# The scan's inverse in 128-token tiles: carrying a transposed product beside the partial inverse, and emptying its banks on two engines

## Chip, cores and metric

One core of a Trainium2 chip (trn2). The metric is the device time of the whole program in microseconds, the median of three runs; lower is better. TensorE is called PE below, VectorE DVE, ScalarE ACT, GpSimd POOL, SyncE SP.

## The reference, cut to what matters

The program is two model blocks on 1024 tokens of width 1024. The change lies in one stage of the first block, a delta-rule scan over tokens with 16 heads of 64, run forward and backward:

```python
def step(S, inp):
    w_t, k_t, v_t, kk_t, b_t = inp[:5]
    sa = jnp.einsum('bhvk,bhk->bhv', S, kk_t)
    S = (S * w_t[:, :, None, :] - sa[..., None] * b_t[:, :, None, :]
         + v_t[..., None] * k_t[:, :, None, :])
    o = jnp.einsum('bhvk,bhk->bhv', S, inp[5]) if with_out else None
    return S, o
...
for d, (lw, la) in enumerate(...):
    S, o = rwkv7_scan(rh, heads(w), kd, vh, kk, heads(a), S0[d], reverse=(d == 1))
```

The kernel doesn't step through the tokens. It takes tiles of 128 tokens; inside a tile the recurrence is a unit-triangular system of 128 equations per head, whose matrix `tri` is the identity plus the masked products of b and kk. It needs the inverse of `tri`, applied to two right-hand sides, and passes a 64x64 state from tile to tile.

## The kernel before, in words

The stage is the function `rwkv`. It works through 8 pairs of heads (i, `HP`), and for each pair 5 units (n): unit 0 is the context tokens (no output needed), units 1 to 4 the 1024 tokens. A unit takes two tiles for each of two directions (x = 0 forward, 1 backward), so with two heads there are 4 matrices of 128x128 per direction (q = 0 to 3), side by side in one [128, 4, 128] buffer, or in one PSUM bank of 512 columns. A direction owns four of the eight banks (0 to 3 of `bank(x, b)`). There are 40 units, (i, n).

**The levels.** The inverse is built by doubling. `lev0` to `lev6` are constant masks with 1 on the diagonal and -1 in the off-diagonal blocks of size 2^m. Y starts as `tri` masked by lev0 (the inverse of the 2x2 blocks), and X as its transpose. A level m = 1 to 6 does, for each direction:

- `g` (PE, bank 0): G = Mr'X, with Mr a rounded copy of `tri`;
- `join` (DVE, L1529): Gs = bank 0 times the mask lev m, rounded to fp32r;
- `x_next` (PE, bank 1), not in the last level: X = Y'Gs, then `x_out` (ACT, L1182) copies it to X;
- `y_next` (PE, bank 2): Y = Gs'Y, then `y_out` (ACT, L1186) copies it to Y.

Each product is `quad`: four matmuls (L1308), 128 columns wide, with a weight load each. A level is so 24 matmuls over both directions, 2 joins and 4 copies. PE's order within a level is g(0), y_next(1) of the level before, g(1), x_next(0), y_next(0), x_next(1).

**Between the levels of two units** (called the transition below) PE has, in this order: `turn_kv` for the next unit's keys and values (L1260, L1262), the last `y_next` of both directions with `turn_ab` (L1271, L1273), `solve` (Y' times the right-hand sides), `gram_b`, `product` (residual with the unrounded `tri`), `gram_k`, `refine` (one correction with Y), `start` for the next unit (L1299: transpose of Y0 into bank 1; L1302: MakV), `g` of the next unit's level 1, then `passing` (L1380) and the products that pass the state and give the output. DVE has in this order: `masks_b` (L1516, L1518), `residual` (L1533), `masks_k` (L1523, L1525), `refined` (L1537, L1538), `join` of level 1, `passed` (L1544, L1545), `state` (L1551) and, for n > 2, `out` (L1557). ACT has keys_out (L1165), the last y_out, pairs_out, solved, start_out (L1176 the first X; L1178 AMv), and for n = 1, 2 an output copy (L1196). POOL makes Y0 (L1123), Mr (L1124) and Rr (L1127).

**Tails.** The finishing of pair i-1 is spread over pair i. PE does `mean` after level 1 of unit 0 and `variance` after level 1 of unit 1 (L1237, two products of 512 columns each). DVE does `center` (L1489) in level 3 of unit 0, `spread` (L1494) in level 3 of unit 1, `normal` (L1499) in level 2 and `affine` (L1504) in level 4 of unit 2. In the last pair DVE also rotates the first keys of the next stage: one `turn` piece (two 128x512 products, L1576 to L1583) in each of levels 2 to 5 of units 2, 3 and 4.

The order on each engine is written out by hand; engines meet in semaphores (`Marks`: `done` counts, `wait` waits for a named point). An engine serves its list strictly in order.

Of the kernel before, what the change touches and what calls it, by code (L numbers as in the profile page):

```python
# [22 lines left out]
P = 128  # L23
# [930 lines left out]
def rwkv(nc, G, proj, Xd, oa, v_tok, rope):  # L954
# [15 lines left out]
    with nc.cleanup_on_exit(), ExitStack() as ctx:  # L970
# [41 lines left out]
        spare = lambda h: bank(h, 3)  # L1012


        lev = range(1, LEVELS)
        last = LEVELS - 1

        def front_names(n):
            xs = n > 0
            return {"pe": ["T1", "T0", "gB", "gK", "XT", "MakV"], "act": ["Ktok", "Vtok", "Atok", "Btok", "X0", "AMv"],  # L1020
                    "dve": ["tri", "MrbT", "MakT", "MrkT"] if xs else ["tri", "MakT"], "pool": ["Y0", "Mr", "AMr"]}

        def level_names(n):
            xy = sum(([f"X{m}", f"Y{m}"] if m < last else [f"Y{m}"] for m in lev), [])
            return {"pe": sum(([f"G{m}", f"X{m}", f"Y{m}"] if m < last else [f"G{m}", f"Y{m}"] for m in lev), []),
                    "act": xy, "dve": [f"G{m}" for m in lev]}

        def back_names(n):
            xs = n > 0
            return {"pe": ["C0", "MC", "XR", "GQ", "Z0"] + (["O0"] if xs else []) + (["Z1"] if n < 4 else []) + (["O1"] if xs else []),  # L1030
                    "act": ["C0"] + (["O"] if n in (1, 2) else []),
                    "dve": ["R", "W", "nY"] + (["GT"] if xs else []) + ["QT", "S0"] + (["S1"] if n < 4 else []) + (["O"] if n > 2 else [])}

        def marks(kind, names):
            return [{e: Marks(nc, None, f"b_{e}_{kind}{x}", sum(([f"{n}.{q}" for q in names(n)[e]] for n in range(5)), []))
                     for e in names(0)} for x in range(2)]
        F, L, B = marks("front", front_names), marks("level", level_names), marks("back", back_names)
        pe_t = Marks(nc, None, "b_pe_tail", ["mu", "var"])
# [17 lines left out]
        with nc.Block() as block:  # L1056
# [95 lines left out]
            def _(act):  # L1152
# [78 lines left out]
            def _(pe):  # L1231
# [18 lines left out]
                def turn_kv(i, n, x):  # L1250
# [6 lines left out]
                    if i_ >= 0:  # L1257
                        L[x]["act"].wait(pe, i_, f"{n_}.X{last - 1}")
# [52 lines left out]
                def g(i, n, x, m):  # L1311
                    if m == 1:
                        F[x]["act"].wait(pe, i, f"{n}.AMv")
                        F[x]["pool"].wait(pe, i, f"{n}.Mr")
                    else:
                        L[x]["act"].wait(pe, i, f"{n}.X{m - 1}")
                    L[x]["pe"].done(quad(bank(x, 0), Mr[x], X[x]), f"{n}.G{m}")

                def x_next(i, n, x, m):
                    L[x]["dve"].wait(pe, i, f"{n}.G{m}")  # L1320
                    if m > 1:
                        L[x]["act"].wait(pe, i, f"{n}.Y{m - 1}")
                    L[x]["pe"].done(quad(bank(x, 1), Y0[x] if m == 1 else Y[x], Gs[x]), f"{n}.X{m}")

                def y_next(i, n, x, m):
                    i_, n_ = before(i, n)
                    if m == 1 and i_ >= 0:
                        B[x]["dve"].wait(pe, i_, f"{n_}.S1" if n_ < 4 else f"{n_}.S0")
                    if m == last:
                        L[x]["dve"].wait(pe, i, f"{n}.G{m}")  # L1330
                        L[x]["act"].wait(pe, i, f"{n}.Y{m - 1}")
                    L[x]["pe"].done(quad(bank(x, 2), Gs[x], Y0[x] if m == 1 else Y[x]), f"{n}.Y{m}")

                def levels(i, n):
                    for m in lev:
                        if m > 1:
# [13 lines left out]

# [122 lines left out]
            def _(dve):  # L1473
# [1965 lines left out]
```

How the kernel before makes its waits and increments, by code:

```python
    def wait(self, back=0):  # L68
        self.eng.wait_ge(self.sem, self.it * self.per + (self.base + self.n - back))
# [48 lines left out]
    def load(self, eng, src, i, per, l, split=False):  # L118
        if split:
            eng.wait_ge(self.cut, i * per + (self.split_base + l + 1))
        else:
            eng.wait_ge(self.free, i * per + (self.base - self.split_base + l + 1))
        b = (self.base + l) % NBUF
        eng.dma_start(self.buf[:, b], src).then_inc(self.full[b], 16)
# [1 line left out]
    def landed(self, eng, i, per, l):  # L127
        n = self.base + l
        eng.wait_ge(self.full[n % NBUF], i * (16 * per // NBUF) + 16 * (n // NBUF + 1))
        return self.buf[:, n % NBUF]
# [1 line left out]
    def split_hi(self, act, l):  # L133
        n = self.split_base + l
        raw = self.landed(act, 0, 0, l)
        act.wait_ge(self.begun, n + 1)
        self.nc.scalar.activation(self.hl[:, n % NBUF, 0], raw, ACT.Copy).then_inc(self.hi_done, 1)
# [1 line left out]
    def split_lo(self, dve, l):  # L140
        n = self.split_base + l
        hi, lo = self.hl[:, n % NBUF, 0], self.hl[:, n % NBUF, 1]
        dve.wait_ge(self.hi_done, n + 1)
        self.nc.vector.tensor_tensor(lo, self.buf[:, (self.base + l) % NBUF], hi.bitcast(F32), ALU.subtract).then_inc(self.cut, 1)
# [1 line left out]
    def split_first(self, eng, scalar):  # L147
# [6 lines left out]
            self.nc.scalar.activation(hi, raw, ACT.Copy).then_inc(self.hi_done, 1)  # L154
        else:
            eng.wait_ge(self.hi_done, n + 1)
            self.nc.vector.tensor_tensor(lo, raw, hi.bitcast(F32), ALU.subtract).then_inc(self.cut, 1)
```

## Time and profile before

| | |
|---|---|
| Median of 3 runs | 4833.94 us (4833.16 to 4834.51) |
| The profiled execution's span | 4830.5 us |
| Its time outside the span | not shown; the span is 3.4 us under the median |
| Busy, whole program | PE 4675.5 us (97%), DVE 2558.1 (53%), ACT 1869.7 (39%), POOL 429.0 (9%) |
| Granted TensorE clock | full in nearly all of 40 slices, nine tenths in three |
| The scan's stage | 1369.5 to 2750, 1380.5 us for 40 units |

A matmul's record covers the time from its issue to its modelled end, about 0.28 us for 128 columns, and the next is issued before that; so the busy share of PE hides gaps, and the distance between issues is what a product costs. A line x4 of the timeline is four merged instructions: its duration less that of one, divided by three, is the distance of the issues.

### The profile page before, as it was taken

What the parts mean: (1) busy time and instruction counts of PE and PEld (TensorE: products, weight loads), DVE (VectorE), ACT (ScalarE), POOL (GpSimd) and SP (SyncE); (2) the same over time, 40 slices, a digit from 0 to 9 for tenths busy, and PEclk for the clock granted to TensorE, in tenths of its full rate; (3) what the DMA queues carried; (4) which work ended last, traced back from release to release, by engine and by line L of the source; (5) the groups of instructions that cost most, each with busy time, mean ns of one, the idle gap of its engine ahead of it and who ended that gap; (6) DMA issues with size and microseconds to landing.
All of it is one profiled execution on the core that took longest, in us unless ns stands there. A gap on an engine that the chain in (4) does not pass through costs nothing. (4 is left out here: it accounts for less than half of the span.)

```text
span 4830.5 us, 68919 instructions
## 1 busy us (share of the span) xinstructions
PE 4675.5 (97%) x28888; PEld 3832.5 (79%) x28888; DVE 2558.1 (53%) x3722; ACT 1869.7 (39%) x3164; POOL 429.0 (9%) x347
## 2 busy tenths in 40 slices
PE   7999999999999999999999899899999779999999
PEld 5888777778999999999999744488777557888887
DVE  3245555446535555555555577555443755555543
ACT  3234443445435554555455434311333753111111
POOL 0000000000022322232222100000010000000000
PEclk9999999999989999999999899999999899999999
DMA  5333434344410110110112154333120021121222
GB/s 204 115 138 140 145 131 154 138 147 153 148 60 19 41 55 28 57 44 23 61 40 84 35 160 126 125 119 140 48 84 26 14 109 53 70 74 70 87 105 92
DMA packets 155988, 441.93 MB, mean 91 GB/s; under 512 B 17169, under 2 KB 47121, under 8 KB 140449
## 3 DMA queue, kind: packets, MB, share of 16 engines
q1 hardware_dynamic: 140624, 383.98, 22.7%
q0 software_dynamic: 9296, 32.58, 1.9%
q10 hardware_dynamic: 5760, 20.97, 1.2%
q8 instruction: 230, 3.77, 0.3%
q14 instruction: 78, 0.63, 0.0%
HBM read 294.86 MB, written 141.56 MB: 90 GB/s over the span
## 5 line engine op out<-in xcount | busy, mean ns | idle before, releaser
L202 PE MATMUL pr_ps<-uhl,w_split 128*128 128x512 f32 (+1 forms) x1520 | 586.0, 385 | 3.1 <-DVE w_split L145 2.2
L206 PE MATMUL pr_ps<-uhl,w_split 128*128 128x512 f32 (+1 forms) x1520 | 571.3, 376 | 0.0
L205 PE MATMUL pr_ps<-uhl,w_split 128*128 128x512 f32 (+1 forms) x1520 | 570.5, 375 | 0.0
L1529 DVE TENSOR_TENSOR b_G<-b_ps,cst 128x512 fp32r<-128x512 f32 x480 | 331.6, 692 | 358.4 <-PE b_ps L1308 357.8
L138 ACT ACTIVATE w_split<-share 128x2048 fp32r<-128x2048 f32 x64 | 122.6, 1915 | 699.4 <-DVE ou_vc L3264 271.1
L202 PEld LDWEIGHTS pr_ps<-uhl,w_split 128*128 128x128 f32 x1520 | 286.7, 189 | 81.5 <-issue 29.2
L205 PEld LDWEIGHTS pr_ps<-uhl,w_split 128*128 128x128 f32 x1520 | 286.8, 189 | 56.1 <-issue 5.8
L206 PEld LDWEIGHTS pr_ps<-uhl,w_split 128*128 128x128 f32 x1520 | 286.6, 189 | 52.7
L1182 ACT ACTIVATE b_X<-b_ps 128x512 fp32r<-128x512 f32 x400 | 240.1, 600 | 213.7 <-PE b_ps L1308 211.4
L1186 ACT ACTIVATE b_Y<-b_ps 128x512 fp32r<-128x512 f32 x480 | 286.8, 598 | 83.2 <-PE b_ps L1308 83.1
L1308 PE MATMUL b_ps<-b_X,b_Mr 128*128 128x128 f32 x1920 | 313.9, 287 | 1.0
L1308 PE MATMUL b_ps<-b_G,b_Y 128*128 128x128 f32 x1920 | 307.3, 287 | 1.6 <-DVE b_G L1529 1.3
L1308 PE MATMUL b_ps<-b_Y,b_G 128*128 128x128 f32 x1920 | 302.2, 281 | 0.3 <-DVE b_G L1529 0.3
L202 PE MATMUL ou_ps<-ou_a,w_split 128*128 128x512 f32 x704 | 277.0, 393 | 7.7 <-DVE ou_a L2119 7.7
L1123 POOL TENSOR_TENSOR b_Y<-b_tri,cst 128x512 fp32r<-128x512 f32 x80 | 101.8, 1273 | 2001.6 <-DVE b_tri L1516 2001.6
L205 PE MATMUL ou_ps<-ou_a,w_split 128*128 128x512 f32 x704 | 275.2, 391 | 0.0
L206 PE MATMUL ou_ps<-ou_a,w_split 128*128 128x512 f32 x704 | 275.2, 391 | 0.0
L202 PE MATMUL mx_ps<-mx_a,w_split 128*128 128x512 f32 x640 | 259.3, 405 | 13.5 <-DVE mx_a L2119 13.5
L1308 PEld LDWEIGHTS b_ps<-b_G,b_Y 128*128 128x128 f32 x1920 | 253.6, 194 | 22.0 <-issue 15.9
L1308 PEld LDWEIGHTS b_ps<-b_X,b_Mr 128*128 128x128 f32 x1920 | 258.7, 195 | 14.2 <-issue 6.7
L1308 PEld LDWEIGHTS b_ps<-b_Y,b_G 128*128 128x128 f32 x1920 | 259.8, 196 | 0.5 <-DVE b_G L1529 0.5
L776 DVE COPY pr_stage<-pr_ps 128x256 f32<-128x256 f32 (+1 forms) x92 | 49.7, 540 | 391.8 <-PE pr_ps L206 391.6
(490 smaller groups left out, 10088.8 us busy)
## 6 DMA issues: line engine op xcount, KB each, us to landing
w_ring<-in_w_in SPq DMA_DIRECT2D x41, 1024.0 KB, 5.3
proj<-pr_stage SPq DMA_DIRECT2D x160, 256.0 KB, 2.0
share<-in_w_up SPq DMA_DIRECT2D x24, 1024.0 KB, 4.7
ar<-share SPq DMA_DIRECT2D x32, 512.0 KB, 2.8
b_AR<-ar SPq DMA_DIRECT2D x64, 256.0 KB, 2.9
pr_raw<-proj SPq DMA_DIRECT2D x48, 256.5 KB, 3.5
ada<-in_ada_w SPq DMA_DIRECT2D x24, 512.0 KB, 5.6
ff<-ou_vc ACTq DMA_DIRECT2D x24, 512.0 KB, 2.6
```

What stands on the lines that cost most here:

```text
L138: self.nc.scalar.activation(self.hl[:, n % NBUF, 0], raw, ACT.Copy).then_inc(self.hi_done, 1)
L202: mm = nc.tensor.matmul(dst, a[0], b[0], start=start, stop=False)
L205: nc.tensor.matmul(dst, a[0], b[1], start=False, stop=False)
L206: return nc.tensor.matmul(dst, a[1], b[0], start=False, stop=stop)
L776: V.tensor_copy(dst, src).then_inc(taken[1], 1)
L1123: F[x]["pool"].done(tt(Y0[x][:], tri[x][e][:], rep(K("lev0"), 4), ALU.mult), f"{n}.Y0")
L1182: L[x]["act"].done(A(X[x][:], heads(x, 1), ACT.Copy), f"{n}.X{m}")
L1186: L[x]["act"].done(A(Y[x][:], heads(x, 2), ACT.Copy), f"{n}.Y{m}")
L1308: mm = mmul(bk[:, q * P:(q + 1) * P], lhsT[:, q], rhs[:, q], start=True, stop=True)
L1529: L[x]["dve"].done(V.tensor_tensor(Gs[x][:], heads(x, 0), rep(K(f"lev{m}"), 4), ALU.mult), f"{n}.G{m}")
```

## The change

X is no longer kept. In its place E, a product in transposed form, is kept beside Y in one buffer `EY` [128, 4, 2, 128], so that one matmul with 256 moving columns advances both. Gs gets two buffers. A level m = 1 to 4 is then, for each direction:

- `f`: F = E'Gs (128 columns, bank 0; for m = 0 with Mr in place of E), which the next `join` masks into the other Gs;
- `ey`: [E, Y] = Gs'[E, Y] (256 columns, banks 1 and 2; heads 0 and 1 in bank 1, heads 2 and 3 in bank 2);
- bank 1 is copied out by ACT (`low`), bank 2 by DVE (`high`).

Level 5 is F5 and Y5 alone, level 6 is Y6. The transition gets a join of level 0 (from bank 1, after L1299's transpose, which now takes Mr), F0 and E0 in place of `g`, and ACT copies E0 in place of X. POOL makes Mr first and Y0 afterwards, the latter once the previous unit's `refine` has read Y.

```diff
-        X = [sb(f"X{x}", [P, 4, P], F32R) for x in range(2)]
-        Y0 = [sb(f"Y0{x}", [P, 4, P], F32R) for x in range(2)]
-        Y = [sb(f"Y{x}", [P, 4, P], F32R) for x in range(2)]
-        Gs = [sb(f"G{x}", [P, 4, P], F32R) for x in range(2)]
+        EY = [sb(f"EY{x}", [P, 4, 2, P], F32R) for x in range(2)]
+        E, Y = [t[:, :, 0] for t in EY], [t[:, :, 1] for t in EY]
+        Gs = [[sb(f"G{x}{b}", [P, 4, P], F32R) for b in range(2)] for x in range(2)]
...
+        both = lambda x: ps[:, 4 * x + 1:4 * x + 3].rearrange("p b (q a f) -> p (b q) a f", q=2, a=2)
...
+        high_on_dve = lambda x: True
...
                     for x in range(2):
                         F[x]["dve"].wait(pool, i, f"{n}.tri")
-                        F[x]["pool"].done(tt(Y0[x][:], tri[x][e][:], rep(K("lev0"), 4), ALU.mult), f"{n}.Y0")
                         F[x]["pool"].done(ts(Mr[x][:], tri[x][e][:], 1.0, None, ALU.mult), f"{n}.Mr")
+                    for x in range(2):
+                        i_, n_ = before(i, n)
+                        if i_ >= 0:
+                            B[x]["pe"].wait(pool, i_, f"{n_}.XR")
+                        F[x]["pool"].done(tt(Y[x], tri[x][e][:], rep(K("lev0"), 4), ALU.mult), f"{n}.Y0")
...
-                def x_out(i, n, x, m):
-                    L[x]["pe"].wait(act, i, f"{n}.X{m}")
-                    L[x]["act"].done(A(X[x][:], heads(x, 1), ACT.Copy), f"{n}.X{m}")
+                def ey_out(i, n, x, m):
+                    L[x]["pe"].wait(act, i, f"{n}.EY{m}")
+                    L[x]["act"].done(A(EY[x][:, 0:2], both(x)[:, 0:2], ACT.Copy), f"{n}.low{m}")
...
+                def f(i, n, x, m):
+                    L[x]["dve"].wait(pe, i, f"{n}.G{m}")
+                    if m == 0:
+                        F[x]["act"].wait(pe, i, f"{n}.AMv")
+                    elif m == 1:
+                        L[x]["act"].wait(pe, i, f"{n}.E0")
+                    else:
+                        L[x]["act"].wait(pe, i, f"{n}.low{m - 1}")
+                    for q in range(4):
+                        if q == 2 and m > 1:
+                            high(x).wait(pe, i, f"{n}.high{m - 1}")
+                        mm = mmul(bank(x, 0)[:, q * P:(q + 1) * P], E[x][:, q] if m else Mr[x][:, q], Gs[x][m % 2][:, q], start=True, stop=True)
+                    L[x]["pe"].done(mm, f"{n}.F{m}")
...
+                    for q in range(4):
+                        mm = mmul(both(x)[:, q], Gs[x][m % 2][:, q], EY[x][:, q], start=True, stop=True)
+                    L[x]["pe"].done(mm, f"{n}.EY{m}")
...
                 def levels(i, n):
-                    for m in lev:
-                        if m > 1:
-                            g(i, n, 0, m)
-                            y_next(i, n, 1, m - 1)
-                            g(i, n, 1, m)
-                        if m < last:
-                            x_next(i, n, 0, m)
-                            y_next(i, n, 0, m)
-                            x_next(i, n, 1, m)
+                    for m in range(1, 6):
+                        for x in range(2):
+                            f(i, n, x, m)
+                            if m < 5:
+                                ey(i, n, x, m)
+                            else:
+                                y_next(i, n, x, m)
                         if m == 1 and i and n == 0:
                             mean(i - 1)
...
                         start(*nxt, 0)
                         start(*nxt, 1)
-                        g(*nxt, 0, 1)
-                        g(*nxt, 1, 1)
+                        for x in range(2):
+                            f(*nxt, x, 0)
+                            e_first(*nxt, x)
                     passing(i, n, 0)
...
+                def high_out(i, n, x, m):
+                    L[x]["pe"].wait(dve, i, f"{n}.EY{m}")
+                    L[x]["dve"].done(V.tensor_copy(EY[x][:, 2:4], both(x)[:, 2:4]), f"{n}.high{m}")
...
-                    for m in lev:
-                        for x in range(2 if m > 1 else 0):
-                            join(i, n, x, m)
+                    for m in range(1, LEVELS):
+                        if m > 1:
+                            for x in range(2):
+                                join(i, n, x, m)
+                            for x in range(2):
+                                if high_on_dve(x) and m < LEVELS - 1:
+                                    high_out(i, n, x, m - 1)
                         if i and (n, m) in tail:
                             tail[n, m](i - 1)
```

## Rows read from the trace of the kernel before

**Rows 1.** Windows, the scan's stage: busy of each engine, clock, DMA share.

```profile
1369.50:2750.00 1380.50, 1372.55 (x13494) 1267.48 (x13495) 750.09 (x1405) 731.15 (x1492) 380.21 (x260) 0.99 0.13 43
```

**Rows 2.** Groups in the stage: line, engine, names, count, busy, mean ns, idle before.

```profile
L1529 DVE TENSOR_TENSOR b_G<-b_ps,cst 128x512 fp32r<-128x512 f32 x480 | 331.6, 692 | 358.4 <-PE b_ps L1308 357.8
L1308 PE MATMUL b_ps<-b_X,b_Mr 128*128 128x128 f32 x1920 | 313.9, 287 | 1.0
L1186 ACT ACTIVATE b_Y<-b_ps 128x512 fp32r<-128x512 f32 x480 | 286.8, 598 | 83.2 <-PE b_ps L1308 83.1
```

**Rows 3.** Timeline of unit (3, 3), from its first product to the next unit's.

```profile
1999.88 0.66 PE L1308 MATMUL b_ps<-b_G,b_Y 128*128 128x128 f32 x4
...
2013.08 0.61 PE L1308 MATMUL b_ps<-b_Y,b_G 128*128 128x128 f32 x4
...
2013.55 0.66 PE L1308 MATMUL b_ps<-b_X,b_Mr 128*128 128x128 f32 x4
...
2014.05 0.40 PE L1260 MATMUL b_ps<-cst,b_Kt 128*128 128x128 f32 x2
...
2014.25 0.69 DVE L1529 TENSOR_TENSOR b_G<-b_ps,cst 128x512 fp32r<-128x512 f32 x1 [0.28 <-PE b_ps L1308]
...
2014.71 1.21 ACT L1165 ACTIVATE b_KV<-b_ps 128x256 f32<-128x256 f32 x4 [0.39 <-PE b_ps L1262]
...
2034.42 0.66 PE L1308 MATMUL b_ps<-b_G,b_Y 128*128 128x128 f32 x4
```

**Rows 4.** Timeline of the projection stage, fp32r matmuls of 256 columns.

```profile
399.74 0.28 PE L202 MATMUL pr_ps<-uhl,w_split 128*128 128x256 f32 x1
399.86 0.28 PE L205 MATMUL pr_ps<-uhl,w_split 128*128 128x256 f32 x1
```

**Rows 5.** Groups by form: DVE copies of 128x512, out of PSUM and within SBUF.

```profile
L776 DVE COPY pr_stage<-pr_ps 128x512 f32<-128x512 f32 x40 | 27.7, 691 | 218.5 <-PE pr_ps L206 218.5
L1478 DVE COPY b_tri<-cst 128x512 f32<-128x512 f32 x2 | 0.8, 422 | 0.0
```

**Rows 6.** Timeline of the transition after unit (3, 3).

```profile
2026.26 0.42 DVE L1538 SCALAR_TENSOR_TENSOR b_WN<-b_ps,b_C 128x256 f32<-128x256 f32 x1
...
2027.21 1.33 PE L1308 MATMUL b_ps<-b_X,b_Mr 128*128 128x128 f32 x8
...
2028.47 1.52 PE L1380 MATMUL b_ps<-b_MB,b_WN 128*64 128x192 f32 x16
```

**Rows 7.** Timeline of `variance` and `center`; groups of the tails and turns on DVE.

```profile
1930.56 1.93 PE L1237 MATMUL b_ps<-b_osq,cst 128*128 128x512 f32 x4
...
1932.72 0.61 PE L1308 MATMUL b_ps<-b_Y,b_G 128*128 128x128 f32 x4
...
1904.29 1.28 DVE L1489 SCALAR_TENSOR_TENSOR b_o<-b_ps,b_o 128x512 f32<-128x512 f32 x2
...
L1499 DVE TENSOR_TENSOR b_o<-b_o,b_osq 128x1024 f32<-128x1024 f32 x7 | 8.5, 1215 | 0.0
L1504 DVE TENSOR_SCALAR b_o<-b_o,par 128x1024 f32<-128x1024 f32 x7 | 5.6, 804 | 0.0
L1580 DVE TENSOR_TENSOR turn_q<-turn_q,share 128x512 f32<-128x512 f32 x4 | 2.7, 686 | 0.0
```

**Rows 8.** Timeline in units (0, 0) and (7, 2); windows around a fall of the clock.

```profile
1378.11 0.69 DVE L1529 TENSOR_TENSOR b_G<-b_ps,cst 128x512 fp32r<-128x512 f32 x1 [2.77 <-PE b_ps L1308]
...
1383.22 0.69 DVE L1529 TENSOR_TENSOR b_G<-b_ps,cst 128x512 fp32r<-128x512 f32 x1 [2.72 <-PE b_ps L1308]
...
2655.49 0.66 PE L1308 MATMUL b_ps<-b_G,b_Y 128*128 128x128 f32 x4 [0.92 <-DVE b_G L1529]
...
1374.80:1402.10 27.30, 27.30 (x131) 27.30 (x130) 7.46 (x13) 12.68 (x23) 1.23 (x1) 0.50 0.04 17
...
2654.40:2658.20 3.80, 2.88 (x25) 2.73 (x25) 3.49 (x6) 2.13 (x5) 0.00 (x0) 1.00 0.00 0
2658.20:2671.80 13.60, 13.24 (x64) 13.06 (x64) 9.57 (x11) 6.37 (x13) 5.43 (x2) 0.50 0.01 1
```

More of the change, by code:

```diff
@@ L1012, in rwkv, with front_names, level_names, back_names @@
         spare = lambda h: bank(h, 3)
-        lev = range(1, LEVELS)
+        both = lambda x: ps[:, 4 * x + 1:4 * x + 3].rearrange("p b (q a f) -> p (b q) a f", q=2, a=2)
         last = LEVELS - 1
-        def front_names(n):
+        def front_names(n, x):
             xs = n > 0
[L1020 to L1028, printed above, removed]
+            return {"pe": ["T1", "T0", "gB", "gK", "XT", "MakV"], "act": ["Ktok", "Vtok", "Atok", "Btok", "AMv"],
+                    "dve": ["tri", "MrbT", "MakT", "MrkT"] if xs else ["tri", "MakT"], "pool": ["Mr", "Y0", "AMr"]}
+        high_on_dve = lambda x: True
+        def level_names(n, x):
+            return {"pe": ["F0", "E0"] + sum(([f"F{m}", f"EY{m}"] for m in range(1, 5)), []) + ["F5", "Y5", "Y6"],
+                    "act": ["E0"] + sum(([f"low{m}"] + ([] if high_on_dve(x) else [f"high{m}"]) for m in range(1, 5)), []) + ["Y5", "Y6"],
+                    "dve": ["G0", "G1"] + sum(([f"G{m}"] + ([f"high{m - 1}"] if high_on_dve(x) and m < LEVELS - 1 else []) for m in range(2, LEVELS)), [])}
+        def back_names(n, x):
             xs = n > 0
@@ L1034, in marks @@
         def marks(kind, names):
-            return [{e: Marks(nc, None, f"b_{e}_{kind}{x}", sum(([f"{n}.{q}" for q in names(n)[e]] for n in range(5)), []))
-                     for e in names(0)} for x in range(2)]
+            return [{e: Marks(nc, None, f"b_{e}_{kind}{x}", sum(([f"{n}.{q}" for q in names(n, x)[e]] for n in range(5)), []))
+                     for e in ("pe", "act", "dve", "pool") if e in names(0, x)} for x in range(2)]
         F, L, B = marks("front", front_names), marks("level", level_names), marks("back", back_names)
+        high = lambda x: L[x]["dve" if high_on_dve(x) else "act"]
         pe_t = Marks(nc, None, "b_pe_tail", ["mu", "var"])
@@ L1201, in _ @@
                     start_out(0, 0, x)
+                for x in range(2):
+                    e_first(0, 0, x)
                 for i, n in UNITS_B:
                     nxt = after(i, n)
-                    for m in range(1, last):
+                    for m in range(1, 5):
                         for x in range(2):
-                            x_out(i, n, x, m)
-                            y_out(i, n, x, m)
+                            ey_out(i, n, x, m)
+                    for x in range(2):
+                        y_out(i, n, x, 5)
                     if nxt:
@@ L1257, in turn_kv @@
                     if i_ >= 0:
-                        L[x]["act"].wait(pe, i_, f"{n_}.X{last - 1}")
+                        L[x]["act"].wait(pe, i_, f"{n_}.low4")
                     for t in range(2):
@@ L1296, in start @@
                     F[x]["dve"].wait(pe, i, f"{n}.MrkT" if n else f"{n}.MakT")
-                    F[x]["pool"].wait(pe, i, f"{n}.Y0")
+                    F[x]["pool"].wait(pe, i, f"{n}.Mr")
                     for q in range(4):
-                        mm = mmul(bank(x, 1)[:, q * P:(q + 1) * P], Y0[x][:, q], ident_r[:], start=True, stop=True)
+                        mm = mmul(bank(x, 1)[:, q * P:(q + 1) * P], Mr[x][:, q], ident_r[:], start=True, stop=True)
                     F[x]["pe"].done(mm, f"{n}.XT")
@@ new lines, in e_first, with ey @@
+                def e_first(i, n, x):
+                    L[x]["dve"].wait(pe, i, f"{n}.G0")
+                    L[x]["pe"].done(quad(bank(x, 1), Gs[x][0], Mr[x]), f"{n}.E0")
+                def ey(i, n, x, m):
+                    i_, n_ = before(i, n)
+                    if m == 1:
+                        F[x]["pool"].wait(pe, i, f"{n}.Y0")
+                        if i_ >= 0:
+                            B[x]["dve"].wait(pe, i_, f"{n_}.S1" if n_ < 4 else f"{n_}.S0")
+                    for q in range(4):
+                        mm = mmul(both(x)[:, q], Gs[x][m % 2][:, q], EY[x][:, q], start=True, stop=True)
+                    L[x]["pe"].done(mm, f"{n}.EY{m}")
@@ L1370, in refine @@
                     B[x]["dve"].wait(pe, i, f"{n}.R")
-                    B[x]["pe"].done(quad(bank(x, 3), Y[x], Gs[x]), f"{n}.XR")
+                    B[x]["pe"].done(quad(bank(x, 3), Y[x], Gs[x][1]), f"{n}.XR")
                 def passing(i, n, x):
@@ L1462, in _ @@
                         start(*nxt, 1)
-                        g(*nxt, 0, 1)
-                        g(*nxt, 1, 1)
+                        for x in range(2):
+                            f(*nxt, x, 0)
+                            e_first(*nxt, x)
                     passing(i, n, 0)
@@ L1587, in _ @@
                         step(0, 0, x)
-                for x in range(2):
-                    join(0, 0, x, 1)
+                for m in range(2):
+                    for x in range(2):
+                        join(0, 0, x, m)
                 for i, n in UNITS_B:
@@ L1612, in _ @@
                     if nxt:
-                        for x in range(2):
-                            join(*nxt, x, 1)
+                        for m in range(2):
+                            for x in range(2):
+                                join(*nxt, x, m)
                     for x in range(2):
```

45 lines of the change are left out of this document (20 added, 25 removed).

## The prediction, made before the changed kernel ran

> **What bounds the kernel now.** I read the windows by stage first: the scan takes 1380.5 us of the 4830.5 us span, and PE is busy in 1372.6 of it, DVE in 750.1, ACT in 731.2 [rows 1]. PE's busy time hides its gaps, so the groups come next: PE waited 1.0 us in all before its G products, DVE 357.8 us for PE before its joins, ACT for PE too [rows 2]. PE is the bound and both readers of PSUM have slack. The timeline gives the step: the first product of unit (3, 3) is issued at 1999.88, the keys' transposes at 2014.05, the next unit's first product at 2034.42 [rows 3]. So a unit takes 34.54 us, of which the levels take 14.17 and the transition 20.37. The 14.17 us hold 30 groups of four products, 0.472 us each, so a level of six groups takes 2.83 us. A group that nothing stalls takes 0.47 or less (2013.08 to 2013.55); from (0.61 - 0.28) / 3 the issues are 0.11 us apart, 0.45 us for four [rows 3].
>
> **Prices.** Narrow product (128 columns): 0.112 us, above. Wide product (256 columns): no such row in this stage; the projection has fp32r products of 256 columns 0.12 us apart [rows 4], with the same 128x128 weights. Above it lies two narrow ones, 0.224. I take 0.12, the row of the very form; four take 0.48. Join: 0.692 us; ACT's copy of a bank: 0.598 [rows 2]. DVE's copy of a bank (`high`): none in this stage. The nearest rows are a DVE copy of 512 columns out of PSUM, 0.691, and one within SBUF, 0.422 [rows 5]. I take 0.69, since the new copy reads PSUM, and keep 0.42 as the lower end. From the start of a group to the start of its reader it is 0.70 us (2013.55 to 2014.25 [rows 3]); 0.65 where its four issues aren't stalled. From a reader's end to PE I take 0.07.
>
> Of a wide product the Trainium skill has the opposite (TensorE: Matmul & The Clock Gate, Back-to-back issue gap): 134 cycles for 128 columns and 262 for 256, so two narrow ones would cost no more than a wide one. By that the merge would save PE nothing. The trace disagrees: 0.11 against 0.12 us.
>
> **The new level.** PE: two narrow and two wide groups, 2 x 0.45 + 2 x 0.48 = 1.86 us instead of 2.83. ACT: two copies, 1.2 us. DVE: two joins and two copies, 4 x 0.69 = 2.76 us, in the order join 0, join 1, high 0, high 1. So DVE becomes the bound. The chain through it, from the end of high 0: 0.07, then the last two narrow products of F for direction 0 (0.22), its wide group (0.48), F of direction 1 until its reader starts (0.65), join 1 (0.69), high 0 (0.69): 2.80 us. Both limits meet there. A level costs 2.80 against 2.83: one third of PE's work is gone and nearly nothing is gained, and PE stands idle 0.94 us in one piece in each level, between F's second and third product.
>
> **The stretch of levels.** From the first product as 0: F1 and EY1 of direction 0 until 0.93, F1 of direction 1 read at 1.58, join 2 of direction 1 until 2.27, high 0 until 2.96. Three more periods: 11.36. Then 0.07 + 0.22 and three groups of 0.45 (Y5, F5, Y5): 13.00, against 14.17, so 1.17 us saved; it comes from the two missing groups at the end (level 6 has no product but Y6) and from the 2.83. ACT's keys_out (2014.71, four copies, then the last two Y [rows 3]) now waits for both Y5 copies, which end at 13.8, 0.15 later against PE than before; the pairs behind it are what `gram_b` waits for. Saved: 1.02.
>
> **The transition.** DVE gets two joins of level 0 behind `refined`, whose last instruction starts at 2026.26 [rows 6] and, with these starting 0.33 apart, hands over at 2026.60. Join 0 ends at 2027.29, F0 can start at 2027.36 (before: G at 2027.21), and then F0, E0, F0, E0 take 1.80: `passing` starts at 2029.16 instead of 2028.47. That is 0.69 later, with the state's chain, S, DVE's `out` and the next unit behind it. PE's XT waits for Mr instead of Y0, which POOL makes first; Y0 now waits for `refine` and is ready some 7 us before EY1 reads it. POOL's move costs nothing as long as that holds. No DMA is moved. Net per unit: -1.02 + 0.69 = -0.33, in 40 units -13 us.
>
> **Unit (0, 0)** runs its levels at half clock: 5.11 us a level [rows 8], so a product takes 5.11 / 24 = 0.213. There the new chain is 0.07 + 0.43 + 0.87 + 1.09 + 1.38 = 3.84 us; four periods save 5 us.
>
> **The tails.** They lay in DVE's slack, and that cover is gone. `center` and `spread` take 1.28 us each, `normal` 1.22, `affine` 0.80 [rows 7], nearly all of it on the path now: 2 x 1.24 + 1.94 = 4.4 us for each of 7 pairs. Against it, `mean` and `variance` took PE 1.71 us each (1930.56 to 1932.72 less one group [rows 7]), and 0.95 of each now falls in PE's idle time. Sum: 7 x (4.4 - 1.9) = +18 us. The turns of the last pair are two instructions of 0.69 [rows 7] in each of 12 levels: +4.1 us each in units 3 and 4, +3 in unit 2, where DVE was already stalled: +11.
>
> So the queues alone give -13 - 5 + 18 + 11 = +11 us.
>
> **The clock.** In unit (7, 2) PE was kept waiting once, from about 2654.40 (its last issue) to 2655.49, by joins behind a tail and a turn; from 2658.2 on the granted clock was 0.5 of full, 1.2 GHz, for 13.6 us, until the levels were over [rows 8]. In unit (0, 0) too the fallen clock stayed for the levels (1374.8 to 1402.1). Otherwise the stage has 1.0, with hardly a gap. The new kernel has a gap of 0.94 us in every level, and of 2.2 us where a tail stands. I expect the clock to fall in the 21 units with tails, for some two levels each, and in part of the other 19, one level each on average: 61 levels. A level at half clock costs 3.84 instead of 2.80: 61 x 1.04 = +63 us. In the last three units the turns' DVE time covers it. Bounds: no level, 0; all 200, +208.
>
> The Trainium skill has a rule that speaks against the change (same page, A second HAM failure mode: psum-queue depth-cycling): short idles of the engine between groups of matmuls are enough to make the clock swing between its two levels. The fall in unit (7, 2) agrees.
>
> **The sum.** +11 + 63 = +74 us on the profiled 4830.5 us span; the median stands 3.4 us above that span, and I add to the median: 4833.9 + 74 = **4908 us**. Its own range, 25 to 150 levels at half clock: 4865 to 5000.
>
> **Rivals.**
> - *The clock holds* (0.16): 4833.9 + 11 = 4845 us, itself uncertain by 15. For it: 0.94 us is shorter than the one gap that was followed by a fall. Against it: there are some 4 per unit, and longer ones.
> - *Faster, by a cheap copy* (0.08): DVE's `high` costs 0.42 like the copy within SBUF. The chain is then 2.53 us, four levels save 1.1 us per unit, 43 us in all: 4845 - 43 = 4802, with less idle and a held clock. It decides when the copy takes under about 0.56 (4 x 40 x 0.13 = 21 us brings 4845 under 4824). Against it: the PSUM row. The Trainium skill agrees with that row (VectorE: DVE Perf Modes, Why PSUM operands drop a tier): a float32 operand in PSUM gets no fast mode.
> - *The half clock sticks in all levels* (0.07): 4845 + 40 x 5 x 1.04 less what the last pair hides: about 5040.
> - *The merge doesn't do what it says* (0.05): the wide product costs two narrow ones, +0.42 in the chain, four levels, 40 units: +67 on 4845, 4912, with PE dense and the clock held.
>
> **Chances.** The likeliest, half clock in part of the levels, has 0.64. What a measurement of this kernel can tell from no change is about 0.2%, 10 us: 4824 to 4844. Faster: 0.08 for the cheap copy and 0.02 of the held clock, 0.10. Within: 0.06 of the held clock. Slower: the rest, 0.84. The range leaves out the cheap copy, the stuck clock and a corner of the held clock: 4838 to 4990.
>
> **What would show it.** Joins of one direction 2.80 us apart in a plain unit; DVE idle before them near zero and PE waiting for `high` of DVE; 0.12 between the wide products; the copy at 0.69; `passing` 0.7 us later after `refined`; levels with `center` 1.2 us longer; and windows of the levels with a clock under 1.0. I am wrong if PE still waits for nothing (a DVE price too high), if the clock is 1.0 throughout (4845), or if a unit is shorter than 34.2 us.

## The result and the profile after

The changed kernel takes **4865.05 us**, median of 4 runs (4863.04 to 4868.26), against 4834.23 for the kernel before on the same chip (4 runs, 4833.16 to 4839.85): ratio 1.0064, 95% interval 1.005 to 1.0078. So it is 31 us slower; forecast were 74, with a range of 4838 to 4990 us, in which the time lies. The profiled execution took 4863.73 us with a span of 4861.9, against the 4830.5 of before: 31.4 us more, and that is what is split up below.

The windows view of the scan's stage (columns: stretch, length, busy of PE, PEld, DVE, ACT and POOL, granted clock, DMA share, GB/s):

```profile
1369.50:2780.00 1410.50, 1311.71 (x12139) 1184.56 (x12138) 971.01 (x1796) 534.20 (x1092) 383.21 (x261) 0.93 0.13 43
```

Against [rows 1]: PE's busy time fell by 61 us, the stage got some 30 us longer (33.2 up to its last unit's join 2), the mean clock fell from 0.99 to 0.93. The groups, after, against [rows 2]:

```profile
L1556 DVE TENSOR_TENSOR b_G<-b_ps,cst 128x512 fp32r<-128x512 f32 x560 | 379.8, 687 | 101.9 <-PE b_ps L1336 100.0 <-PE b_ps L1313 1.0
L1336 PE MATMUL b_ps<-b_G,b_EY 128*128 128x128 f32 x1600 | 301.8, 300 | 93.5 <-DVE b_EY L1560 78.1 <-DVE b_G L1556 13.6
L1350 PE MATMUL b_ps<-b_EY,b_G 128*128 128x256 f32 x1280 | 235.7, 309 | 0.0
L1560 DVE CAST b_EY<-b_ps 128x512 fp32r<-128x512 f32 x320 | 204.3, 679 | 0.0
L1189 ACT ACTIVATE b_EY<-b_ps 128x512 fp32r<-128x512 f32 x320 | 191.1, 597 | 381.5 <-PE b_ps L1350 381.5
```

The roles are turned, as forecast. PE now waits for DVE before F's products (93.5 us; before, 1.0), mostly for `high` (L1560). DVE's idle time before joins fell from 358 us to 102, and before `high` it has none: each copy finds its data ready and starts late because it stands in DVE's queue. ACT idles 381 us.

One level of a plain unit, timeline of unit (3, 3):

```profile
2011.29 0.69 DVE L1556 TENSOR_TENSOR b_G<-b_ps,cst 128x512 fp32r<-128x512 f32 x1 [0.23 <-PE b_ps L1336]
...
2011.89 1.28 DVE L1560 CAST b_EY<-b_ps 128x512 fp32r<-128x512 f32 x2
...
2012.63 0.44 PE L1336 MATMUL b_ps<-b_G,b_EY 128*128 128x128 f32 x2 [0.59 <-DVE b_EY L1560]
...
2012.90 0.69 PE L1350 MATMUL b_ps<-b_EY,b_G 128*128 128x256 f32 x4
2013.11 0.69 DVE L1556 TENSOR_TENSOR b_G<-b_ps,cst 128x512 fp32r<-128x512 f32 x1
...
2013.43 0.56 PE L1336 MATMUL b_ps<-b_G,b_EY 128*128 128x128 f32 x4
```

This is the forecast chain, link by link, from start to start. Join 1 to `high` 0: 0.60 (forecast 0.69). `high` 0 to PE: 0.74 (0.76). Two narrow products: 0.27 (0.22). Wide group: 0.53 (0.48). F of direction 1 to the next join 1, which starts at about 2014.03: 0.60 (0.65). Sum **2.74 us against 2.80**. Before it took 2.83. A plain unit takes 33.96 us instead of 34.54, 0.58 less; forecast were 0.33 less.

A level with a tail: DVE and two rows of PE in unit (2, 0), timeline, and then the windows of its stalls, of the fall and of what came after:

```profile
1719.45 1.28 DVE L1560 CAST b_EY<-b_ps 128x512 fp32r<-128x512 f32 x2
1720.65 1.27 DVE L1513 SCALAR_TENSOR_TENSOR b_o<-b_ps,b_o 128x512 f32<-128x512 f32 x2
1721.84 1.27 DVE L1556 TENSOR_TENSOR b_G<-b_ps,cst 128x512 fp32r<-128x512 f32 x2
...
1722.58 0.44 PE L1336 MATMUL b_ps<-b_G,b_EY 128*128 128x128 f32 x2 [0.51 <-DVE b_G L1556]
...
1723.04 1.27 DVE L1560 CAST b_EY<-b_ps 128x512 fp32r<-128x512 f32 x2
...
1723.77 0.44 PE L1336 MATMUL b_ps<-b_G,b_EY 128*128 128x128 f32 x2 [0.76 <-DVE b_EY L1560]
```

```profile
1720.80:1724.20 3.40, 2.13 (x16) 1.79 (x16) 3.40 (x6) 1.20 (x2) 1.89 (x1) 0.99 0.00 0
1724.20:1734.40 10.20, 10.10 (x50) 9.91 (x49) 4.01 (x7) 4.30 (x9) 0.00 (x0) 0.50 0.01 2
1734.40:1750.90 16.50, 16.23 (x178) 14.41 (x178) 11.56 (x24) 4.64 (x11) 8.36 (x6) 1.00 0.00 1
```

Eight DVE instructions run without a pause, 0.60 us from start to start, though each lasts 0.69: DVE is the bound here. `center` (L1513) holds the joins back, PE stalls for 0.51 and 0.76 us, is busy in 2.13 of 3.40 us, and then the clock is at 1.2 GHz for 10.2 us. In pairs 1 to 6 that happened in 14 of the 18 units with tails (three of units 0, all six of units 1, five of units 2) and in none of the 12 without; in pair 0, which has no tails, never. The four units that kept the clock had such stalls too: 0.51 and 0.75 or 0.76 us in units (1, 0), (4, 0) and (6, 0). In all, the stage has some 181 us at 1.2 GHz up to its last unit's join 2, before 41.

**Where the 31.4 us come from.** I took the start of each unit's join 2 from both traces and subtracted. For a unit whose clock had not fallen I took its length; what the fallen ones have more is put to the clock. Unit 1 of pairs 1 to 6 always fell: its length without a fall, 35.62 us, is run 2's 36.11 less the 0.49 that the filler of that run costs in unit 0, an estimate. Pair 7 is split by run 2 too (148.9 us there, 156.1 in this kernel, 144.1 before); in its units 2 and 3 the clock fell in run 2 as well, and before in unit 2, so the +4.8 holds costs of the clock on both sides, and 1 us of filler. Measured without any such step are the pair's +12.0 and, of the 48.9, 28.8 us in units 0 and 2.

| part | forecast | measured |
|---|---|---|
| unit (0, 0) | -5 | -11.4 |
| pair 0, units 1 to 4 | -1.3 | -4.1 |
| pairs 1 to 6 without falls (169.04 us a pair, before 170.85) | +5.1 | -10.9 |
| pair 7 with its turns, as in run 2 | +11.9 | +4.8 |
| falls of the clock (48.9 in pairs 1 to 6, 7.2 more in pair 7 than in run 2) | +63 | +56 |
| stage's first joins (-1.3), from the last unit's join 2 to the next stage (+5.1), behind it (-6.9) | 0 | -3 |
| sum | +74 | +31 |

(The kernel before does `mean` ahead of join 2, the changed one behind it. So 1.7 us of the gain in pair 0's row belong to pair 1, and each pair hands as much to the one before; pair 7's row has no such credit. The sum isn't touched. Of the last row, the 6.9 us behind the scan are no work of the change either: the clock was at 1.2 GHz there for 87.6 us in the one trace and for 101.3 in that of the kernel before.)

### The profile page after: what moved, and what is told of

The parts are those of the page before. It is cut to its first block and busy times, and to the rows that moved or that the text cites. A ratio compares the mean times of both kernels' runs of the same rounds, so it can differ in the third digit from the quotient of the medians.

```text
span 4861.9 us, 66517 instructions
## 1 busy us (share of the span) xinstructions
PE 4616.1 (95%) x27608; PEld 3753.2 (77%) x27608; DVE 2781.0 (57%) x4122; ACT 1673.0 (34%) x2764; POOL 430.2 (9%) x347
## 5 line engine op out<-in xcount | busy, mean ns | idle before, releaser
L1556 DVE TENSOR_TENSOR b_G<-b_ps,cst 128x512 fp32r<-128x512 f32 x560 | 379.8, 687 | 101.9 <-PE b_ps L1336 100.0
L1336 PE MATMUL b_ps<-b_G,b_EY 128*128 128x128 f32 x1600 | 301.8, 300 | 93.5 <-DVE b_EY L1560 78.1
L1336 PEld LDWEIGHTS b_ps<-b_G,b_EY 128*128 128x128 f32 x1600 | 247.6, 209 | 137.0 <-DVE b_EY L1560 101.5
L1189 ACT ACTIVATE b_EY<-b_ps 128x512 fp32r<-128x512 f32 x320 | 191.1, 597 | 381.5 <-PE b_ps L1350 381.5
L1124 POOL TENSOR_SCALAR b_Mr<-b_tri 128x512 fp32r<-128x512 f32 x80 | 117.7, 1489 | 2021.5 <-DVE b_tri L1540 2021.5
L202 PE MATMUL mx_ps<-mx_a,w_split 128*128 128x512 f32 x640 | 258.0, 403 | 13.5 <-DVE mx_a L2156 13.5
L206 PE MATMUL mx_ps<-mx_a,w_split 128*128 128x512 f32 x640 | 255.1, 399 | 0.0
L205 PE MATMUL mx_ps<-mx_a,w_split 128*128 128x512 f32 x640 | 253.7, 396 | 0.0
L1350 PE MATMUL b_ps<-b_EY,b_G 128*128 128x256 f32 x1280 | 235.7, 309 | 0.0
L205 PE MATMUL ou_ps<-ou_ext,w_split 128*128 128x512 f32 x576 | 224.1, 389 | 0.0
L202 PE MATMUL ou_ps<-ou_ext,w_split 128*128 128x512 f32 x576 | 224.1, 389 | 0.0
```

The lines of the kernel that those rows point to most:

```text
L202: mm = nc.tensor.matmul(dst, a[0], b[0], start=start, stop=False)
L205: nc.tensor.matmul(dst, a[0], b[1], start=False, stop=False)
L206: return nc.tensor.matmul(dst, a[1], b[0], start=False, stop=stop)
L1189: L[x]["act"].done(A(EY[x][:, 0:2], both(x)[:, 0:2], ACT.Copy), f"{n}.low{m}")
L1336: mm = mmul(bank(x, 0)[:, q * P:(q + 1) * P], E[x][:, q] if m else Mr[x][:, q], Gs[x][m % 2][:, q], start=True, stop=True)
L1350: mm = mmul(both(x)[:, q], Gs[x][m % 2][:, q], EY[x][:, q], start=True, stop=True)
```

## The experiments

The theory, after this reading: the tails make the clock fall, and cost a little by themselves; the chain through DVE sets the plain level. Rivals: DVE's serial work is the loss and the clock only follows; the gap in every level costs the clock; DVE's total work sets the level. (The letters in the expectations are each text's own.) Experiments 1 to 4 stood beside a kernel before of 4833.6 us (10 runs), 5 to 7 beside 4836.2 (11 runs), 8 and 9 beside 4830.4 (7 runs). From the next stage's first product to the end of the span the traces take between 2051.7 us (the changed kernel) and 2058.5 (the kernel before), though nothing is changed there; so what is worth less than some 7 us is read from the units and not from the time of the whole.

**1. Tails behind the last join.**

```diff
-                tail = {(0, 3): center, (1, 3): spread, (2, 2): normal, (2, 4): affine}
+                tail = {(0, 6): [center], (1, 6): [spread], (2, 6): [normal, affine]}
```

(POOL's last step on the pair moves from unit 2 to unit 3 with it.)

> The changed kernel with DVE's tails of a pair moved out of the levels: center, spread, normal and affine stand behind the last join of units 0, 1 and 2, where DVE waited some 4 us for the first Gram product; POOL's finish goes one unit later. The turns of the last pair stay in the levels. Theory A (the loss is the clock, which falls where a tail makes PE's gap long): in pairs 1 to 7 no window under 1.0 except in the last pair's units 2 to 4, each unit 1 and 2 of a pair some 4.5 us shorter, the whole kernel 75 to 90 us shorter than the changed one: 4775 to 4795 us, below the kernel before. Rival B (the loss is DVE's serial work, the clock only follows it): only the tails' own DVE time of about 3.8 us a pair comes back, 27 us: 4835 to 4845. Rival C (gaps of 0.9 us in plain levels make the clock fall as soon as its phase allows): falls remain in the plain units, over 4845.

**4792.03 us** (4785.56 to 4793.39), ratio 0.9915 [0.99, 0.9929]. Windows view of this kernel, then of the changed one over the same stretch:

```profile
1370.00:2660.00 1290.00, 1200.02 (x11795) 1079.88 (x11794) 942.71 (x1739) 515.88 (x1066) 370.94 (x254) 0.99 0.14 46
```

```profile
1370.00:2660.00 1290.00, 1202.78 (x11185) 1086.32 (x11184) 883.60 (x1635) 490.95 (x1008) 351.09 (x241) 0.94 0.13 44
```

Same instructions, 73 us less, and the clock stays up in pairs 1 to 6, with PE still waiting 0.58 or 0.59 us in each plain level, as in this row of PE:

```profile
1714.21 0.44 PE L1336 MATMUL b_ps<-b_G,b_EY 128*128 128x128 f32 x2 [0.58 <-DVE b_EY L1560]
```

Both rivals of that text fall: the serial work alone was to give 4835 to 4845 us, the gap of the plain level over 4845. Timeline of DVE in the first levels of unit (2, 0):

```profile
1707.19 1.28 DVE L1560 CAST b_EY<-b_ps 128x512 fp32r<-128x512 f32 x2
1709.21 0.69 DVE L1556 TENSOR_TENSOR b_G<-b_ps,cst 128x512 fp32r<-128x512 f32 x1 [0.75 <-PE b_ps L1336]
...
1711.95 0.69 DVE L1556 TENSOR_TENSOR b_G<-b_ps,cst 128x512 fp32r<-128x512 f32 x1
...
1714.69 0.69 DVE L1556 TENSOR_TENSOR b_G<-b_ps,cst 128x512 fp32r<-128x512 f32 x1
```

Joins of direction 0 are 2.74 apart (1709.21, 1711.95, 1714.69). `mean` is in the level before: the join period there, from 1705.75 to 1709.21, is 3.47, so `mean` costs 0.73 and not 1.71.

**2. The clock held by filling PE.** Tails stay where they are; in units 0 to 2 of pairs 1 to 7 the wide group of direction 1 is issued once more, and twice more in the level ahead of a tail, into the same banks, so that PE has work while it waits.

```diff
-                    for q in range(4):
-                        mm = mmul(both(x)[:, q], Gs[x][m % 2][:, q], EY[x][:, q], start=True, stop=True)
+                    more = 0 if x == 0 or not i or n > 2 else 2 if (n, m) in ((0, 3), (1, 3), (2, 2), (2, 4)) else 1
+                    for _ in range(1 + more):
+                        for q in range(4):
+                            mm = mmul(both(x)[:, q], Gs[x][m % 2][:, q], EY[x][:, q], start=True, stop=True)
```

> The changed kernel with PE's idle time in the levels of the tailed units (pairs 1 to 7, units 0 to 2) filled: direction 1's wide group is issued once more, and twice more in the level before a tail, with the same operands into the same banks, so nothing else changes. Theory A: the clock stays at 1.0 in those units, so their joins lie as far apart as now at full clock (3.5 and 3.9 us at a tail, 2.4 to 2.7 else) and the transitions behind them take 19.8 to 23.0 us instead of up to 26.5; the kernel gets 45 to 60 us shorter than the changed one, 4805 to 4820. Rival B: DVE's serial work is unchanged and PE has more to do, so the same 4865 or up to 10 us more.

**4818.74 us** (4814.56 to 4821.03), ratio 0.9969 [0.9958, 0.998]: more work, 46 us less time than the changed kernel.

```profile
1375.97:2660.00 1284.03, 1216.99 (x11965) 1101.57 (x11965) 915.74 (x1691) 503.82 (x1043) 363.16 (x247) 1.00 0.13 43
```

The clock is at 1.00, with no fall in pairs 1 to 6, and nothing else was taken away. The filler costs 0.49 us in unit 0 of each pair (first join period 3.95 instead of 3.47); with as much in unit 1, where it can't be read off, 7 us in all. So the falls are worth 46 + 7 = 53 us, near the 56 of the table, which is in part made from this same run. The tails' own time is the rest of the 73: 20 us, or 2.9 us a pair: 0.85 for `center` (unit 0 takes 32.38 us with it and 31.53 in run 1), by the estimate of the table the same for `spread`, and 1.19 for the other two.

**3. Both banks emptied by ACT.**

```diff
-        high_on_dve = lambda x: True
+        high_on_dve = lambda x: False
```

> The changed kernel with both banks of EY emptied by ACT in both directions; DVE keeps the joins alone. Theory A (DVE is what a level waits for): ACT's copies start about 0.5 us apart, so ACT needs 2.1 us a level, and the chain high copy, two products, wide group, low copy, high copy is about 2.4 us; a plain level takes 2.35 to 2.5 us instead of 2.74 and the tails lie in DVE's slack again, so the clock holds: 4740 to 4780 us. Rival D (the level is bound by one direction's chain, in which the two copies now stand one behind the other): a level of 2.9 us or more, 4870 to 4900.

**4700.94 us** (4696.19 to 4704.61), ratio **0.9728** [0.9714, 0.9743]; it beats both kernels. The level is 2.14 us, shorter than expected. Groups and a timeline of ACT:

```profile
L1556 DVE TENSOR_TENSOR b_G<-b_ps,cst 128x512 fp32r<-128x512 f32 x560 | 380.3, 689 | 151.4 <-PE b_ps L1336 149.3 <-PE b_ps L1313 0.8
L1336 PE MATMUL b_ps<-b_G,b_EY 128*128 128x128 f32 x1600 | 279.6, 284 | 3.1 <-DVE b_G L1556 2.9
```

```profile
1936.73 0.60 ACT L1189 ACTIVATE b_EY<-b_ps 128x512 fp32r<-128x512 f32 x1
...
1937.23 0.59 ACT L1191 ACTIVATE b_EY<-b_ps 128x512 fp32r<-128x512 f32 x1
...
1937.71 0.60 ACT L1189 ACTIVATE b_EY<-b_ps 128x512 fp32r<-128x512 f32 x1
...
1938.20 0.59 ACT L1191 ACTIVATE b_EY<-b_ps 128x512 fp32r<-128x512 f32 x1
```

PE's wait falls from 93.5 to 3.1 us (this stretch is 1370 to 2660). ACT's copies last 0.60 but start 0.49 apart, so four take 2.0 us, about as expected (2.1). What failed is the chain that I had put at 2.35 to 2.5 us: the level is shorter than that.

**4. Direction 1's `high` on ACT, direction 0's stays on DVE** (`high_on_dve = lambda x: x == 0`).

> The changed kernel with bank 2 emptied by DVE in the forward direction and by ACT in the backward one: three copies of DVE's four and three of ACT's four slots. Theory A: DVE needs 3 x 0.61 = 1.8 us a level and ACT 3 x 0.5 = 1.5, PE's 1.9 and the chain decide: 2.2 to 2.4 us a level, tails partly in the slack, clock held: 4720 to 4760 us. Rival D: the chain of the direction with both copies on ACT decides, as in the kernel with all of it on ACT: the same time as that one, within 5 us.

**4789.86 us** (4787.44 to 4791.54), ratio 0.9914 [0.9897, 0.9931]. DVE, unit (3, 3):

```profile
1976.82 0.69 DVE L1556 TENSOR_TENSOR b_G<-b_ps,cst 128x512 fp32r<-128x512 f32 x1 [0.53 <-PE b_ps L1336]
1977.74 0.69 DVE L1556 TENSOR_TENSOR b_G<-b_ps,cst 128x512 fp32r<-128x512 f32 x1 [0.22 <-PE b_ps L1336]
1978.35 0.68 DVE L1560 CAST b_EY<-b_ps 128x512 fp32r<-128x512 f32 x1
1979.56 0.69 DVE L1556 TENSOR_TENSOR b_G<-b_ps,cst 128x512 fp32r<-128x512 f32 x1 [0.53 <-PE b_ps L1336]
```

My expectation failed: the plain level is still 2.74 us (1976.82 to 1979.56), with a quarter of DVE's work gone. The 75 us come from the tails, which have slack again, and from the clock, which didn't fall in pairs 1 to 6. So it isn't the amount of DVE's work that sets 2.74, but, as it seemed, the place of direction 0's `high` behind join 1, which must itself wait for PE. Runs 5 and 6 put that to the test from two sides.

**5. The order join 0, `high` 0, join 1, `high` 1.**

```diff
                             for x in range(2):
                                 join(i, n, x, m)
-                            for x in range(2):
                                 if high_on_dve(x) and m < LEVELS - 1:
```

> The changed kernel with VectorE's order in a level turned from join 0, join 1, high 0, high 1 to join 0, high 0, join 1, high 1; nothing else. Theory C (what sets a level at 2.74 us is the chain through direction 0's high, which stands behind join 1 and its wait for PE): without that place in the queue the chain is some 1.8 us, and the level is bound by VectorE's four operations at 0.61 us from start to start: 2.44 us. Plain levels 2.44 to 2.52 us, some 0.25 us less in each of 160 levels, 40 us, with a gap of PE that is shorter, so fewer falls of the clock: 4790 to 4825 us. Rival L (VectorE's total work of four operations sets the level, each costing 0.69 from start to start): level 2.74, time within 5 us of the changed kernel's 4865.

**4790.83 us** (4782.13 to 4793.61), ratio 0.9906 [0.9891, 0.9921]. The same four operations. DVE, unit (3, 3):

```profile
1976.79 0.68 DVE L1560 CAST b_EY<-b_ps 128x512 fp32r<-128x512 f32 x1
...
1977.39 0.68 DVE L1556 TENSOR_TENSOR b_G<-b_ps,cst 128x512 fp32r<-128x512 f32 x1
...
1977.98 0.68 DVE L1560 CAST b_EY<-b_ps 128x512 fp32r<-128x512 f32 x1
...
1978.58 0.68 DVE L1556 TENSOR_TENSOR b_G<-b_ps,cst 128x512 fp32r<-128x512 f32 x1
```

No wait is left on DVE, a level is four starts of 0.60: 2.40 us. The rival that total work sets the 2.74 falls: the work is the same. The clock still fell behind tails (some 110 us at 1.2 GHz up to the last unit's join 2), though a plain level has no stall of PE over 0.1 us here. In unit (1, 0) one stall stood 2.3 us ahead of the fall at 1544.7:

```profile
1542.44 0.44 PE L1336 MATMUL b_ps<-b_G,b_EY 128*128 128x128 f32 x2 [0.83 <-DVE b_G L1556]
```

**6. The mirror of 4: direction 0's `high` on ACT, direction 1's on DVE** (`lambda x: x == 1`).

> The mirror of the run with one direction: direction 0's high half is copied by ScalarE, direction 1's by VectorE. VectorE has three operations a level as in that run (join 0, join 1, high 1), and ScalarE three. In that run the level stayed at 2.74 us. Theory C (the chain through direction 0's high, held up behind join 1): here direction 0's high isn't on VectorE, and direction 1's has the whole of direction 0's groups (some 1.05 us of PE) to be ready in, so PE is the bound: level 2.1 to 2.25 us, time 4695 to 4730 us, as with both highs on ScalarE. Rival L (three operations on VectorE, wherever they stand, give the level of that run): 2.74 us, 4785 to 4795 us.

**4712.88 us** (4711.87 to 4714.46), ratio 0.9749 [0.9732, 0.9765]. DVE, unit (3, 3):

```profile
1939.12 0.69 DVE L1556 TENSOR_TENSOR b_G<-b_ps,cst 128x512 fp32r<-128x512 f32 x1
1940.04 0.69 DVE L1556 TENSOR_TENSOR b_G<-b_ps,cst 128x512 fp32r<-128x512 f32 x1 [0.23 <-PE b_ps L1336]
1940.64 0.68 DVE L1560 CAST b_EY<-b_ps 128x512 fp32r<-128x512 f32 x1
1941.26 0.69 DVE L1556 TENSOR_TENSOR b_G<-b_ps,cst 128x512 fp32r<-128x512 f32 x1
```

The level is 2.14 us (1939.12 to 1941.26). The same number of instructions on each engine as in run 4, 77 us apart. In both the copy stands behind join 1, which waits for F of direction 1. Behind that F, PE's list has direction 1's wide group and then at once the reader of direction 0's `high`; the reader of direction 1's `high` comes only after direction 0's F and wide group as well.

**7. The kernel before, with PE busy at the entry of the stage.** For unit (0, 0)'s -11.4: in the kernel before, the clock fell at 1374.8 after PE had waited 1.00 us for POOL, and stayed down for the levels of that unit [rows 8]; in the changed kernel, where POOL makes Mr first and PE waited 0.33 us, it didn't.

```diff
-                    for q in range(4):
+                    for q in list(range(4)) * (3 if (i, n, x) == (0, 0, 0) else 1):
                         mm = mmul(bank(x, 0)[:, q * 64:(q + 1) * 64], MakT[x][:, q], KV[x][e][:, 1, q], start=True, stop=True)
```

> The kernel before, with direction 0's eight products of MakV in unit (0, 0) issued three times instead of once, so that PE is busy through its 1.00 us wait for POOL's Y0 just ahead of the first levels. Nothing else. Theory E (that wait is what the clock fell after at 1374.8, and it then stayed at 1.2 GHz for 27 us of unit (0, 0)): the levels of unit (0, 0) run at full clock, a level 2.83 instead of 5.11 us, time 4833.9 - 11 = 4820 to 4826 us. Rival: the earlier wait at the entry of the stage (4.64 us before the first transposes) decides it, and the clock falls for unit (0, 0) all the same: 4832 to 4837 us.

**4820.38 us** (8 runs, 4815.37 to 4822.63), ratio 0.9968 [0.9957, 0.9978]. Windows of this kernel, where [rows 8] had 0.50:

```profile
1374.80:1380.00 5.20, 5.08 (x44) 4.80 (x43) 1.53 (x4) 1.72 (x4) 5.19 (x4) 1.00 0.94 388
...
1390.00:1402.00 12.00, 12.00 (x104) 10.98 (x105) 6.07 (x11) 7.13 (x17) 3.29 (x3) 1.00 0.00 1
```

Unit (0, 0), from join 2 to join 2, takes 31.39 us instead of 42.19. So the 11 us that the change gained here need no merge: eight more small products (sixteen in the records, which show each twice) give 10.8 us of them to the old kernel too. That POOL's order is what kept the clock up in the changed kernel is likely but not shown. The whole is 16 us shorter by the medians and 11.5 by the traces, but the sum is made otherwise: the entry of the stage takes 2.9 us more, the fall in unit (7, 2) costs 3.0 more, and 6.6 us come from behind the last unit's join 2, where nothing was changed.

**8. Runs 5 and 1 together** (order, and tails late).

> Two edits together: VectorE's order join 0, high 0, join 1, high 1, and the tails behind the last join of units 0, 1 and 2. Theory: they act on different things and both stay. The late tails alone gave 4792 (no falls of the clock, no tails between joins), the order takes another 0.34 us (2.74 to 2.40) off four periods of each of the 37 units that aren't in the last pair's turns, and shortens the tailed periods too: 4792 - 37 x 1.3 = 4744, range 4735 to 4760 us. Rival: both win by the same thing (less idle time of PE, so the clock), and together give what one gives: 4780 to 4792 us.

**4729.02 us** (4725.88 to 4731.7), ratio 0.9787 [0.9773, 0.9802]. Both gains stay, and it is 6 us under the range I gave: a plain unit takes 32.31 us, 1.65 less than in run 1 and not 1.3, since the order shortens the end of the levels too.

**9. Both highs on ACT, tails late** (runs 3 and 1).

> Both highs on ScalarE, as in that earlier run, and the tails behind the last joins as well. Theory: with VectorE at two joins a level of 2.14 us the tails stood in its slack again (no falls of the clock in pairs 1 to 6), so moving them changes nothing in the levels: within 6 us of the 4701 of both highs on ScalarE, 4695 to 4707. Rival: each tail still delays a join by up to 0.6 us, and the move takes 7 x 2 us off: 4683 to 4690 us.

**4694.67 us** (4693.93 to 4696.05), ratio 0.9717 [0.9701, 0.9733]. As expected nearly nothing over run 3; units 0, 1 and 2 of pairs 1 to 6 are as long in both (29.8, 33.1 and 31.7 us), so in run 3 the tails are wholly in slack. In the trace of run 3 the clock fell in unit (7, 2), which took 39.8 us, here 32.0. Fastest of all.

## Why the prediction was right and wrong

**Right: the bound, the chain, the sign.** DVE takes PE's place, PE waits for `high` in each level, the merge takes a third of PE's products and gives back next to nothing. Wide products are really cheaper than two narrow ones: 0.13 us against 0.22 (0.53 for the group of four). (The figures that the prediction took from the Trainium skill for this (TensorE: Matmul & The Clock Gate, Back-to-back issue gap), 134 and 262 cycles, would by my estimate make two narrow ones 2% dearer than a wide one, not quite "no more".) The copy lasts 0.679, as [rows 5] said for PSUM.

**Wrong: "the queues alone give +11 us".** They gave -25: the table's rows but the clock's, with the estimates named there. That is 36 of the 43 us. The prediction's own sign came true: a unit shorter than 34.2 us. (Its own range also begins too low: 25 levels at half clock give 4871 and not 4865.) Four terms of it:

- *DVE per instruction.* I used durations (0.69) where an engine with a full queue is meant; starts are 0.60 apart. This was to be read from the rows of before: `center`'s two instructions took 1.28 us together [rows 7], which is 0.60 + 0.68. It makes the chain 2.74 and not 2.80, some 10 us over 39 units (0.58 gained in each and not 0.33), and leaves DVE 0.34 us of slack in each plain level (2.74 less 2.40).
- *The tails.* "Nearly all of it on the path now", 4.4 us a pair: measured 2.9, some 10 us over 7 pairs. A tail shifts the joins by 1.19, but the next level takes that slack back: `center` costs 0.85.
- *`mean` and `variance`.* I took 0.76 of 1.71 us each as remaining; it is 0.73 (3.47 less 2.74) and 0.81. This was right.
- *Unit (0, 0).* I kept its half clock. It rose, -11.4 instead of -5 (run 7 shows what hung on it). The turns of pair 7 were too dear as well: 4.8 for the pair by that split and not 11.9. That this has the reason of the first point is my reading; no run takes the turns out.

**The clock: the sum near by luck, the places wrong.** Forecast: 61 levels at half clock, 42 of them in units with tails and 19, one each, in the others, +63 us. Measured +56 us, most of it taken away by run 2 alone, but all of it in units with tails or turns; the 0.59 us gap of the plain level (I had said 0.94) never made the clock fall, in any of the 12 tail-free units of pairs 1 to 6 or in pair 0. In return 8 of the 14 falls in pairs 1 to 6 lasted 10.2 or 13.7 us, longer than the two levels that I had given each, and into the transition, where PE is dense and pays in full. What the Trainium skill tells of another kernel (TensorE: Matmul & The Clock Gate, A second HAM failure mode: psum-queue depth-cycling), that frequent brief idles between groups of matmuls make the clock swing, happened here behind tails and not in the plain levels.

**The rivals.** "The clock holds" gave 4845; run 2 is nearly that case, 4812 without its filler. "Cheap copy" (4802) had the wrong mechanism: the copy took 0.679 us. That runs 1 and 2, with the falls gone, stand at 4792 and 4819 is no support for it.

**Where the gain went.** PE's saved third is 0.97 us a level by the prediction's count (2.83 less 1.86). Of it 0.09 came through. Direction 0's `high` behind join 1 holds 0.34 (run 5), DVE's four starts another 0.26 (2.40 to the 2.14 of run 3). I did not test what keeps run 3 at 2.14 rather than at 1.86.

## What to carry to other kernels

Cost a full queue by the distance from start to start, not by the duration of one. When work moves onto an engine, see where in its order the new instruction stands: one that is ready, behind one that waits, costs as much as a slow one (runs 4 and 6: same work, 77 us). The idle engine was a good place for all of it: the Trainium skill advises both ScalarE and VectorE for emptying PSUM (TensorEngine Tiling (Array Packing), PSUM Bottleneck), but here ScalarE alone was 2.7% faster than the kernel before and this split 0.6% slower, as VectorE had the joins and the tails already. Other splits did well: direction 1's `high` alone on VectorE (run 6) was 2.5% faster, and the same split in another order with late tails (run 8) 2.1%.

## What was not expected of the hardware

A stall on PE of some 0.6 us in every plain level left the granted clock at 1.0 all through pairs 0 to 6 of run 1 (1375 to 2537 us), while two stalls of 0.5 and 0.8 us on top of it, behind one tail, were followed by 1.2 GHz for 7 to 14 us, though not each time: 4 of 18 units with tails kept the clock. In run 5 one stall of 0.83 us behind a tail was enough, with next to none in the other levels. What decides it stays open. More PE work, useless in itself, made the kernel 46 us faster. Copies of 128x512 out of PSUM that follow one another start 0.60 us apart on DVE (0.68 long) and 0.49 on ACT (0.60 long).
